# Cross attention of a hybrid block: logits on the unnormalised q, the norm moved into the exponential's scale

## The reference, cut to what matters

```python
def rms_norm(x, g):
    y = xf * lax.rsqrt(jnp.mean(xf * xf, axis=-1, keepdims=True) + EPS)
    return (y * g.astype(jnp.float32)).astype(x.dtype)

def memory_cross_attention(h, mem_n, wq, wkv, q_g, k_g, wo):
    q = rms_norm((h @ wq).reshape(b, s, XA_HEADS, XA_HEAD_DIM), q_g)
    kv = mem_n @ wkv
    k = rms_norm(kv[..., :XA_WIDTH].reshape(b, m, XA_HEADS, XA_HEAD_DIM), k_g)
    v = kv[..., XA_WIDTH:].reshape(b, m, XA_HEADS, XA_HEAD_DIM)
    logits = jnp.einsum("bshd,bmhd->bhsm", q, k) * (XA_HEAD_DIM ** -0.5)
    p = jax.nn.softmax(logits, axis=-1)
    o = jnp.einsum("bhsm,bmhd->bshd", p, v).astype(h.dtype)
    return o.reshape(b, s, XA_WIDTH) @ wo
```

## Time and profile before

| | |
|---|---|
| time, median of 3 runs | 1870.1 us (1869.51 to 1877.01) |
| the profiled execution's own time | 1880.2 us |
| its span, first to last instruction | 1878.4 us |
| TensorE (PE) matmul busy | 1698.0 us, 90% |
| TensorE weight loads (PEld) busy | 1387.5 us, 74% |
| VectorE (DVE) busy | 1054.6 us, 56% |
| ScalarE (ACT) busy | 627.5 us, 33% |
| GpSimd (POOL) busy | 181.0 us, 10% |
| mean granted TensorE clock | 0.950 |

### The profile page before, as it was taken

One profiled execution on the slowest core, in us unless ns is written; L12 is line 12 of the kernel. 1 busy time (PEld: TensorE's weight loads), 2 busy tenths in 40 slices (PEclk: granted clock), 3 DMA queues, 4 the chain that ended last, 5 costly groups with the idle time before them and its releaser, 6 DMA issues.

```text
span 1878.4 us, 22537 instructions
## 1 busy us (share of the span) xinstructions
PE 1698.0 (90%) x7738; PEld 1387.5 (74%) x7738; DVE 1054.6 (56%) x1446; ACT 627.5 (33%) x893; POOL 181.0 (10%) x98
## 2 busy tenths in 40 slices
PE   3596898666889799999999999999999999999996
PEld 3485677565578678888888788888878888888885
DVE  5939957793446474423443576766744554444333
ACT  2202125212223353323432444555422344344221
POOL 6786400231000000000000000000000000000000
PEclk9798878898689999999999999999999999999998
DMA  5222100001002122332233233333322222222332
GB/s 194 79 89 78 45 6 1 1 0 34 1 12 79 45 74 94 99 103 90 89 101 95 72 102 91 91 102 91 96 97 92 90 101 89 100 91 89 96 96 75
DMA packets 43623, 144.11 MB, mean 77 GB/s; under 512 B 4672, under 2 KB 5824, under 8 KB 43584
## 3 DMA queue, kind: packets, MB, share of 16 engines
q1 hardware_dynamic: 42240, 140.62, 23.4%
q10 hardware_dynamic: 1344, 2.98, 0.5%
HBM read 141.23 MB, written 2.10 MB: 76 GB/s over the span
## 4 chain that ended last, share of the span: by engine, by line
PE 81%; DVE 12%; issue 4%; ACT 2%; DVEq 1%; DMA 0%; ACTq 0%; SPq 0%
PE acc L563 72%; DVE qkv L1589 1%; DVE tok L1756 1%; PE acc L700 1%; PE acc L640 1%; DVE c_acc L1565 1%; PE acc L835 1%; DVE sqacc L1479 1%; DVE d_score_a L1761 1%; DVE m_sqa L1479 1%; DVE d_score_b L1761 1%; PE acc L847 0%; PE acc L807 0%; PE acc L590 0%; PE acc L796 0%
## 5 line engine op out<-in xcount | busy, mean ns | idle before, releaser
L563 PE MATMUL acc<-h_hi,w_hi 128*128 128x512 f32 x1280 | 506.1, 395 | 24.0 <-DVE proj L1578 24.0
L563 PE MATMUL acc<-h_hi,w_lo 128*128 128x512 f32 x1280 | 507.2, 396 | 0.0
L563 PE MATMUL acc<-h_lo,w_hi 128*128 128x512 f32 x1280 | 506.2, 395 | 0.0
L1497 DVE TENSOR_TENSOR w_lo<-raw,w_hi 128x1024 fp32r<-128x1024 f32 (+1 forms) x244 | 285.2, 1172 | 85.8 <-ACT w_hi L1109 64.7
L1109 ACT ACTIVATE w_hi<-raw 128x1024 fp32r<-128x1024 f32 (+1 forms) x244 | 245.2, 1008 | 184.8 <-PE acc L563 101.3
L563 PEld LDWEIGHTS acc<-h_hi,w_hi 128*128 128x128 f32 x1280 | 243.2, 190 | 82.7 <-issue 28.4
L563 PEld LDWEIGHTS acc<-h_lo,w_hi 128*128 128x128 f32 x1280 | 243.3, 190 | 57.0 <-issue 1.5
L563 PEld LDWEIGHTS acc<-h_hi,w_lo 128*128 128x128 f32 x1280 | 243.2, 190 | 50.3
L1861 DVE TENSOR_TENSOR x<-x,acc 128x512 f32 x32 | 22.0, 688 | 150.5 <-PE acc L563 150.5
L563 PE MATMUL acc<-u_hi,w_lo 128*128 128x512 f32 x256 | 100.9, 394 | 0.0
L563 PE MATMUL acc<-u_lo,w_hi 128*128 128x512 f32 x256 | 100.4, 392 | 0.0
(11 more groups left out here) (344 smaller groups left out, 2423.5 us busy)
## 6 DMA issues: line engine op xcount, KB each, us to landing
raw<-panels_a SPq DMA_DIRECT2D x112, 512.0 KB, 3.2
raw<-panels_b SPq DMA_DIRECT2D x68, 512.0 KB, 3.2
raw<-mix SPq DMA_DIRECT2D x48, 448.0 KB, 3.3
raw<-mix SPq DMA_DIRECT2D x16, 512.0 KB, 3.6
raw<-down SPq DMA_DIRECT2D x16, 384.0 KB, 3.1
raw<-down SPq DMA_DIRECT2D x16, 320.0 KB, 2.9
x<-xT ACTq DMA_DIRECT2D x1, 2048.0 KB, 13.4
outT<-x SPq DMA_DIRECT2D x8, 256.0 KB, 2.1
```

Of the source, the lines that this page charges most:

```text
L563: mm = e.matmul(out, w[:, w_at:w_at + wn], a, start=first and n == 0, stop=last and n == 2)
L1497: TTn(lo, raw, k.w_hi[:, ahead.slot(w)].bitcast(F32), ALU.subtract).then_inc(k.s_split_done, 1)
```

## The change

The logits are made from q as it was evicted, with neither its norm nor its weight vector. The weight vector is folded into the keys (`xa_q * xa_k`, a new 128x1 product before L1532). The inverse norm of q, which depends on the token only, becomes the per-partition scale column of the exponential, and the factor 1/sqrt(128) goes into it too: the root is now of the sum of squares plus 128 EPS, not of their mean plus EPS. The maxima are scaled by minus that column. The rows of step 3 and the four products of step 4 are gone, with their semaphore.

```diff
@@ plan_memory
     k.eps, _ = sb("eps", 4)
+    k.xa_qk, _ = sb("xa_qk", 1)
@@ tensor_program
     token_sums(4, [til(k.a_p, h) for h in range(HEADS)])
-    e.wait_ge(k.s_unit_inv, GRP_AQ)
-    for h in range(HEADS):
-        row(4 + h, TOK_RG + TT * h)
     e.wait_ge(k.s_xk_done, 1)
     def logits(h):
-        e.wait_ge(k.s_aq_done, h + 1)
+        e.wait_ge(k.s_aq_raw, h + 1)
...
         if h >= 2:
             e.wait_ge(k.s_ao_lo_done, h - 1)
-        else:
-            e.wait_ge(k.s_aq_done, h + 1)
...
-    e.wait_ge(k.s_aq_done, HEADS)
@@ scalar_program
-    def unit_root(group, bank, at, n, scale):
+    def unit_root(group, bank, at, n, scale, eps=k.eps[:, 0:1]):
         e.wait_ge(k.s_unit_sum, group + 1)
-        A(k.tok[:, at:at + n], k.ps[bank][:, 0:n], ACT.Sqrt, bias=k.eps[:, 0:1], scale=scale).then_inc(k.s_unit_std, 1)
+        A(k.tok[:, at:at + n], k.ps[bank][:, 0:n], ACT.Sqrt, bias=eps, scale=scale).then_inc(k.s_unit_std, 1)
...
-    unit_root(GRP_AQ, 4, TOK_RG, HEADS * TT, 1.0 / P)
+    unit_root(GRP_AQ, 4, TOK_RG, HEADS * TT, 1.0, k.eps[:, 3:4])
...
                 ins = A(k.a_p[:, at:at + MEM], k.ps[half][:, n * MEM:(n + 1) * MEM], ACT.Exp,
-                        scale=XA_SCALE, bias=k.tok[:, TOK_NM + t_:TOK_NM + t_ + 1],
+                        scale=k.tok[:, TOK_RG + TT * h + c:TOK_RG + TT * h + c + 1],
+                        bias=k.tok[:, TOK_NM + t_:TOK_NM + t_ + 1],
                         accum_out=k.tok[:, TOK_SUM + t_:TOK_SUM + t_ + 1])
@@ vector_program
+    e.memset(k.eps[:, 3:4], P * EPS)
...
+    TTn(k.xa_qk[:, 0:1], col(k, "xa_q"), col(k, "xa_k"), ALU.mult)
     chain(e.reciprocal(xk_r, xk_r))
-    STT(out=k.xk[:], in0=k.xk[:], scalar=col(k, "xa_k"), in1=xk_r, op0=ALU.mult, op1=ALU.mult).then_inc(k.s_xk_done, 1)
+    STT(out=k.xk[:], in0=k.xk[:], scalar=k.xa_qk[:, 0:1], in1=xk_r, op0=ALU.mult, op1=ALU.mult).then_inc(k.s_xk_done, 1)
...
     unit_inverse(GRP_AQ, TOK_RG, HEADS * TT)
-    for h in range(HEADS):
-        e.wait_ge(k.s_unit_row, ROW_AQ + h + 1)
-        q = til(k.a_q, h)
-        STT(out=q, in0=q, scalar=col(k, "xa_q"), in1=k.ps[4 + h][:], op0=ALU.mult, op1=ALU.mult).then_inc(k.s_aq_done, 1)
...
-            TS(tok(TOK_NM + t_, 2), tok(TOK_MX + t_, 2), -XA_SCALE, None, ALU.mult).then_inc(k.s_al_max, 1)
+            STT(out=tok(TOK_NM + t_, 2), in0=tok(TOK_MX + t_, 2), scalar=-1.0,
+                in1=tok(TOK_RG + TT * h + 2 * half, 2), op0=ALU.mult, op1=ALU.mult).then_inc(k.s_al_max, 1)
```

More of the change, by code:

```diff
@@ L91 @@
 GRP_G, GRP_DQ, GRP_C, GRP_GO, GRP_AQ = 1, 2, 3, 4, 5
-ROW_DQ, ROW_C, ROW_G, ROW_GO, ROW_AQ = 0, 3, 4, 12, 16
+ROW_DQ, ROW_C, ROW_G, ROW_GO = 0, 3, 4, 12
 class Count:
@@ L367, in signals @@
     k.s_aq_raw = sem("aq_raw")
-    k.s_aq_done = sem("aq_done")
     k.s_al_mm = sem("al_mm")
@@ L1447 @@
 GELU_SCALE = 2.0 * 0.7978845608028654
-XA_SCALE = 128 ** -0.5
 PAN_S6 = 112
```

## The result

Before: 1869.8 us median (1869.32 to 1877.01, 4 runs). Changed: **1899.0 us** median (1894.18 to 1900.72, 4 runs). The ratio is 1.0143, 95% interval 1.0111 to 1.0175. The forecast was 1866.5 us and no measurable change; the range 1861 to 1873 does not hold the time.

The account below looks back on a forecast made before the run. TensorE was taken to bound everything behind the attention, passing its gain to the end. Head 0's 4.7 us less 1.1 us for heads 1 to 3 gave 3.6 us, hence 1866.5 us, range 1861 to 1873.

Parts of the forecast that it names:

- no measurable change: Whole kernel: time stays within about 0.5% (9.4 us) of before; chance 0.87.
- Edits at nothing: Third memset, 128x1 product and 32-byte move of later tiles, which all large products read: claimed to cost nothing.
- Rival (d): Large products behind the attention: the 32-byte move is felt, 0.5% on 1200 us, 6 us either way; chance 0.03.
- What bounds the kernel: Behind the attention: TensorE busy 1194.60 of 1201 us, so every microsecond gained in the attention comes out at the end.
- The rows removed: Attention's front: logits(0) starts as the sums end, first half takes 1.92 us, exponentials begin at 628.25 instead of 633.94.
- The scale column: Attention's exponentials: a second column adds 92 ns to each 485 ns, 1.5 us at the most for 16.
- The clock: Attention's front: low clock returns to full at the same moment as before, between 630 and 631 us, within logits(1).
- rival (b): Attention: low clock lasts longer, through logits(1) and the first turn; gain only 2.0 us, 1868.1 us; chance 0.18.
- The size of the gain: Attention: first turn 4.7 us earlier, less 1.1 us given back in heads 1 to 3, a gain of 3.6 us.

Follow-up runs that it names:

- all_shift64: The kernel before with every tile, weight slots included, moved 64 bytes further; ratio 0.9992 (0.9974 to 1.001).
- experiment 3: Changed kernel without the tile shift, its exponentials given an immediate scale and a constant bias column; exponentials 484 ns against 574, no kernel time given.
- imm_scale: Changed kernel without the tile shift, exponentials taking scale 1e-4 and a constant bias column; one execution for durations alone, exponentials 484 ns against 574.
- pad_before_h: The kernel before with 32 unused bytes behind the tile tok, so h and all behind it move; ratio 1.0153 (1.0124 to 1.0182).
- pad_only: The kernel before with one unused 32-byte tile behind eps, moving every later tile; 1903.0 us against 1874.8, ratio 1.017.
- after_noshift: The changed kernel with the new product in a free column of eps, so no tile moves; 1873.3 us, ratio 0.9992 (0.9974 to 1.001).

## Why the prediction was wrong

**The step that failed** is in "Edits at nothing": the new tile moves every later tile by 32 bytes, "so this is nothing too". I took the duration of a pass over `ub_hi`, 394 ns against 0.39 over h. But passes overlap, and what a dense stretch costs is the distance between their starts. Rounded to 0.01 us, as the prediction has it, that distance is 0.23 both before and after. The loss was to be seen in the same trace all the same. The timeline of TensorE before, around the six passes over ub:

```profile
1063.25 0.39 PE L563 MATMUL acc<-h_hi,w_lo 128*128 128x512 f32 x1
1063.48 0.40 PE L563 MATMUL acc<-ub_hi,w_hi 128*128 128x512 f32 x1
1063.72 0.39 PE L563 MATMUL acc<-ub_lo,w_hi 128*128 128x512 f32 x1
...
1064.64 0.40 PE L563 MATMUL acc<-ub_hi,w_lo 128*128 128x512 f32 x1
1064.88 0.40 PE L563 MATMUL acc<-h_hi,w_hi 128*128 128x512 f32 x1
```

From 1063.48 to 1064.88 it is 1.40 us for six, about 233 ns each, where h has 228.9; that is near the 233.3 that the changed kernel then had. (`ub` lay at 32 modulo 256 from the weights and h came to lie at 96; both are long.) So `ub` was no evidence for "nothing", but for a loss. Some 2000 products of three passes (1280 on h, 256 on u and 176 on f in the groups, 288 on the rest by the code) by 13.2 ns are an estimate of 26 us, near the measured ratio: 0.0143 by 1870 = 27 us. In the two profiles only 18.1 us of it shows behind the attention, because the kernel before lost time there itself in that execution, 4.1 us of it in the stretch of 579 passes (last section). Against all_shift64, which has the old attention and the old distance, the five stretches are 23.8 us longer (1206.40 against 1182.64). The 288 products ahead of the attention would add 3.8 if TensorE bounds them too, which was not shown. Rival (d) named the mechanism but gave it 0.03 and 6 us; its price should have been taken from the distance, and since the move was certain and TensorE busy for 1195 of 1201 us, it had to be bounded with care before anything else.

**What bounds the kernel** was right, and it is why a few ns a pass decide: but for pauses of 6.4 us in all nothing covers TensorE behind the attention, and the chain of waits runs on through those.

**The rows removed** was right in its front: logits(0) begins with the end of the sums (625.86 and 625.85), the first half takes 1.93 us (1.92 forecast), the first exponentials come 2.9 us behind the sums (2.8), the table's load is hidden.

**The scale column** was right: 574 ns (577), a round of 6.68 (6.69), 90 ns by experiment 3.

**The clock** was mis-sized. I let it come back at the moment of before, between 630 and 631; in the changed kernel it came back just before 634, so logits(1) takes 3.75 us in the chain of waits (1.97 before) and the first turn starts at 633.83, 14.3 us behind the start of the sums (16.1 before) and not 11.1. It had also fallen earlier, so the sums took 6.36 us. This is rival (b), in a stronger form. And it falls a second time in the last head, a term that the prediction did not have: from the last head's exponentials to the projection it is 11.1 us (648.72 to 659.83), before 9.5 (651.15 to 660.65). That second fall is in all ten traces without the rows, imm_scale with its old rounds among them, and in one of the four with them (pad_before_h). So it does not need the longer exponentials, and it comes more often without the rows, but they do not rule it out. Why stays open: TensorE does the same work there, shifted in time.

**The size of the gain.** From the first sum to the projection the four traces with rows take 39.6 (before), 41.2 (all_shift64), 41.3 (pad_only) and 43.5 us (pad_before_h); the seven without them that have the same order and the scale column take 38.1, 38.1, 38.8, 40.3, 40.3, 40.4 and 40.5. The means are 41.4 and 39.5: a gain of about 1.9 us, where 3.6 was forecast. It is an estimate, since the two groups overlap and the moments at which the clock falls and returns are in it. The timed ratio without the shift, 0.9992 (0.9974 to 1.001), is 1.5 us less with 3.4 either way, which holds both and nothing as well. Had the tile lain in `eps`, the forecast of no measurable change would have been right, and 0.9992 of 1869.8 lies in the range, but that would have said little on the 3.6 us.

## What to carry to other kernels

An edit that adds a tile moves all tiles behind it; where TensorE streams without a pause, put the new tile where nothing moves, or compare the addresses before and after. Read dense matmul stages by the distance between starts (a stretch's length over its count), not by the duration of one. And when an experiment shows that a layout matters, try the other layouts: the best one here was none of the two compared.

## What the runs showed of the hardware that was not expected

- The distance between fp32r passes of 512 columns, each with its own weight load, depends on the addresses of weights and streamed tile against each other, at a granted clock of 1.00: in the stretch of 1512 passes 226.7 ns at a distance of 0 modulo 256 bytes, 228.9 at 64, 233.3 at 32, 96 and 192, 232.4 at 128. Two places 256 bytes apart gave the same at 64 (51776 and 52032 bytes) and at 0 (51968 and 52224); 160 and 224 have only the few passes over `ub`, and steps under 32 bytes were not tried. That the reads of the weights and of the streamed tile meet in the same part of the memory is my guess and was not tried otherwise. The Trainium skill, TensorE: Matmul & The Clock Gate, section "Back-to-back issue gap", has about 216 ns for an isolated 512-column pass and about 131 for a sustained stream, and lets the spacing in a stream depend on the weight load as well, but names no address; the traces here show 226.7 at best and nothing near 131.
- At a distance of 64 both spacings occur, with the same addresses and in the same execution. The kernel before, on either side of the pause of TensorE that ends at 1367.96:

```profile
1362.67 0.39 PE L563 MATMUL acc<-ya_lo,w_hi 128*128 128x512 f32 x1
...
1364.73 0.39 PE L563 MATMUL acc<-ya_lo,w_hi 128*128 128x512 f32 x1
...
1368.98 0.63 PE L563 MATMUL acc<-ya_hi,w_lo 128*128 128x512 f32 x1
1369.41 0.63 PE L563 MATMUL acc<-yb_hi,w_hi 128*128 128x512 f32 x1
...
1371.95 0.40 PE L563 MATMUL acc<-yb_lo,w_hi 128*128 128x512 f32 x1
...
1376.15 0.40 PE L563 MATMUL acc<-ya_lo,w_hi 128*128 128x512 f32 x1
```

  Nine passes in 2.06 us are 228.9 ns each; behind the pause the first are at the low clock, 0.43 apart, and then eighteen take 4.20 us, 233.3 each, and so it goes on to the end of that stretch. This and the low clock make its 136.92 us against 132.82 in after_noshift, which has neither. Of some 1850 groups of three at a granted clock of 1.00, between 3 (all_shift64) and 194 (before) take 700 ns in the six executions at 64; at 96 nearly all do. So the good address allows the short distance and does not ensure it; what decides between the two stays open.
- The kernel's opening moves the time from run to run: TensorE's first pass comes 23.3 us after the start in after_noshift and 30.5 in before, with the same code ahead of it but for one memset. So single profiles of two kernels should be compared stage by stage and not by their spans.
